# Seven products for the queries and keys of the second branch, and another placing of the weight sums

## The chip, the cores and the metric

The kernel runs on one core of one Trainium2 chip. The metric is the device time of one execution in microseconds (us), lower is better. One matmul step of the source (`nc.tensor.matmul` on fp32) stands in the trace as two MATMUL instructions.

## What is computed

Two layers of a transformer-like step on 640 tokens (512 latent, 128 context) of width 1024. Each layer forms modulation vectors, projects the modulated input h with one large matrix, runs three attention branches, gates and merges them, and ends with a mixture of experts. What this case touches:

```python
mod = jax.nn.silu(cvec) @ w_mod_l + b_mod_l            # 6 x 1024 values, twice (context, latent)
h = x * (1.0 + sc1) + sh1
qa, ka, va, qb, kb, vb, qc, kc, vc = split(h @ w_in_l)  # qb, kb: 512 columns each
ga, gb, gc = split(sigmoid(h @ w_gate_l + b_gate_l), 3)
y = (ga * (oa @ w_br_l[0]) + gb * (ob @ w_br_l[1]) + gc * (oc @ w_br_l[2])) @ w_o_l
```

## The kernel before

**Stages.** Per layer, for each branch `br` in 0, 1, 2: `project(br)` (chunks of `h @ w_in`, `CHUNKS`: 2, 0, 1, then 3, 4, 5, then 6, 7), `attend(br)` (18 slots of scores, softmax, transposes and value products) and `merge` (the branch's output product, gated into zT by VectorE at L2519). TensorE fills the gaps of the attention with the products of the gate `h @ w_gate`; `FILL` says how many steps stand in each slot.

**Seven products.** A gate pair has 2 blocks of 128 outputs, 1024 inputs and 640 tokens: halves in each direction, 2 x 2 x 2, so eight products of 4 steps in the plain way. `fill` makes it seven (LOW_LOW, CROSS, HIGH_LOW, DOWN, ACROSS, LATE, HIGH_HIGH, 4 steps of 320 columns each): GpSimd makes sums of token halves (`token_sum`, L1061), VectorE makes four sums of weight quarters per pair (`first_sums`: L2320 to L2322, `last_sum`: L2328) and adds the products from PSUM (`add_products`, L2350 to L2359, one 128x320 instruction or two each). The weights of LATE are made in place in `cross_sum`, once CROSS has read it; the first sums of the next pair wait for LATE.

**Chunks 3 and 4** (queries and keys of branch 1) are computed turned, features on the partitions: `units(c)` is 8, each unit is 8 steps of 320 columns (64 steps a chunk), and ScalarE copies each unit to `QT` or `KT`. Chunk 5 (values) is five units of 8 steps of 512 columns.

**Modulation.** Two groups of 8 pieces of `w_mod` (1 MB each) are summed per layer by VectorE while chunks 3 to 5 run: `modulation_partials`, two passes of 128x2048 a piece (L2368 for the first piece of a group, L2370 for others), 32 in all. After 16 passes TensorE sums the partials over partitions (`sum_partials`, L1246), once after unit (4, 1) and once after (5, 3).

**Order around the change.** SyncE loads 1 MB pieces in program order (L984) into a ring of six slots, each as soon as the piece that held the slot is used; `PROJECT_SLOTS` and `MOD_ORDER` place those of branch 1, and the modulation pieces have two slots. Every engine's own order is written out by hand; an engine waits in order, so what stands behind a waiting instruction waits too. In a slot s of `attend`, VectorE does maxima(s), gate work, the branch's output copy, and the softmax end of s; scores(s + 1) wait for ScalarE's exponentials of s, and the value product of item 1, 5, 9 and 13 waits for the output copy (v_oev) of the unit before.

Of the kernel before, what the change touches and what calls it, by code (L numbers as in the profile page):

```python
# [24 lines left out]
CTX = LAT  # L25
# [30 lines left out]
SIGMOIDS = 3  # L56
PIECE = 2048
# [262 lines left out]
def turned(c):  # L320

    return c in (3, 4)


def units(c):

    return 8 if turned(c) else NT
# [19 lines left out]
def build_kernel(nc, A, OUT):  # L347
# [14 lines left out]
    with ctx:  # L362
# [72 lines left out]
        part_sum = area(26624, 512).rearrange("p (k n) -> p k n", k=4)  # L435
        cross_sum = sb("cross_sum", [128, 4, 128])
        cexp = area(18176, KB * 32).rearrange("p (k n) -> p k n", k=KB)
# [158 lines left out]
        v_sum, g_gated = sem("outputs_summed"), sem("outputs_gated")  # L596
# [29 lines left out]
        class SumsDone:  # L626


            def __init__(self, first, last):
                self.first, self.last, self.done = first, last, [[0, 0] for _ in range(3)]  # L630

            def upto(self, br, n):
                done = self.done[br]
                while True:
                    a, b = done
                    if a > b:
                        if SEVEN * b + CROSS + 1 > n:
                            return
                        self.last(br, b)
                        done[1] += 1  # L640
                    else:
                        if a == PAIRS or (a and SEVEN * (a - 1) + LATE + 1 > n):
                            return
                        self.first(br, a)
                        done[0] += 1
# [315 lines left out]
        for layer in range(DEPTH):  # L961
# [3 lines left out]
            with nc.Block(no_gpsimd_drain=True) as block:  # L965
# [60 lines left out]
                def _(pool):  # L1026
# [35 lines left out]

                    for br in range(3):
# [11 lines left out]
                        if br == 1:  # L1075
# [6 lines left out]
                            if layer == 0:  # L1082
                                zero_row = y_all[0:1, :].rearrange("r (p n) -> (r p) n", p=8)
                                pool.dma_start(zero_row, MB[0:8, 0, MB_ZERO[0]:MB_ZERO[0] + 128]).then_inc(zero_out, 16)
                            for g in range(LAT):
                                masked_bias(0, g)
                            load_bias(1)
                        if br == 2:
                            token_sum(2, 3)
                        for c in CHUNKS[br]:  # L1090
# [11 lines left out]
                            i = PU.index((br, c, CTX))  # L1102
                            typ = CHUNK_TYPE[c]
                            if typ == "k" and turned(c):

                                pool.wait_ge(a_copy, AU.index(PU.index((br, c, units(c) - 1))) + 1)
# [91 lines left out]
                def _(pe):  # L1198
# [40 lines left out]
                    def sum_partials(g):  # L1239
# [4 lines left out]
                        for v in range(2):  # L1244
                            for j in range(STRIPS):
                                last = nc.tensor.matmul(ps[32 * j:32 * j + 32, 6, :], unit_col[:, v, :], mod_acc[:, v, 512 * j:512 * j + 512],  # L1246
# [76 lines left out]

                    def project(br):
                        for n, c in enumerate(CHUNKS[br]):
# [4 lines left out]
                            if layer and br == 0 and n == 0:  # L1330
                                own_outputs(pe, layer - 1)
                                transpose_x(0, 4)
                            for t in range(units(c)):
                                i = PU.index((br, c, t))
                                if br and (n, t) == (0, 2):

                                    pe.wait_ge(v_z, KB * br)
                                if i >= 4:
# [6 lines left out]
                                for k in range(KB):  # L1345
# [10 lines left out]
                                    if turned(c):  # L1356
                                        b, part = divmod(t, 2)
                                        last = mm(ps[:, bank_of(i), 0:320], wk[:, 128 * b:128 * b + 128], hT[:, k, 320 * part:320 * part + 320],
                                                  k == 0, k == KB - 1, frees=k < KB - 1)
                                        continue  # L1360
# [6 lines left out]
                                if (c, t) in MOD_SUMS:  # L1367
                                    sum_partials(1 + MOD_SUMS.index((c, t)) + (layer == 0))
# [1853 lines left out]
```

## Time and profile before

| | us |
|---|---|
| median of 3 runs | 2136.37 (2136.27 to 2140.67) |
| the profiled execution's own time | 2136.38 |
| its span in the trace | 2134.3 |
| TensorE busy (matmul) | 2007.2, 94% |
| VectorE busy | 1292.1, 61% |
| ScalarE busy | 513.9, 24% |
| GpSimd busy | 238.2, 11% |

TensorE is near saturated over the whole span. The mean granted clock of TensorE is 0.984 of full speed. The trace gives each engine's instructions with their start, their length and, in brackets, how long the engine had been idle before and what ended that.

### The profile page before, as it was taken

The numbers are of one execution on the slowest core, as the hardware profiler recorded it, in microseconds if no ns is written. First come the engines' busy times: TensorE is split into PE (matmuls) and PEld (weight loads), VectorE is DVE, ScalarE is ACT, GpSimd is POOL, SyncE is SP. The second block draws the span as 40 slices with busy tenths as digits, with TensorE's granted clock in tenths as the row PEclk, the third lists the DMA queues.
The fourth block names the chain that finished last, engine by engine and source line by source line (L and its number), as shares of the span: only waits on it lengthen the run. The fifth ranks groups of instructions, "written<-read, shape, count | busy, mean of one in ns | idle before, by whom it ended". The sixth has DMA issues, their size and how long they took to land. (4 is left out here: it accounts for less than half of the span.)

```text
span 2134.3 us, 25339 instructions
## 1 busy us (share of the span) xinstructions
PE 2007.2 (94%) x9546; PEld 1173.9 (55%) x9546; DVE 1292.1 (61%) x2031; ACT 513.9 (24%) x1007; POOL 238.2 (11%) x250
## 2 busy tenths in 40 slices
PE   7999999999999999699899999999999999979995
PEld 3457766566467754344244676656755676434432
DVE  2747747675456665756444574776744665866664
ACT  2114401143124400122130342003402342002221
POOL 1000020421110000100120002031101000010003
PEclk9999999999999999899999999999999999989998
DMA  7631046411120061689781111552111105238996
GB/s 284 243 118 40 21 143 222 138 55 44 40 82 21 33 279 79 247 341 362 257 278 48 64 41 64 195 185 87 48 57 46 43 21 221 105 133 322 385 350 199
DMA packets 62682, 317.00 MB, mean 149 GB/s; under 512 B 14824, under 2 KB 15280, under 8 KB 34272
## 3 DMA queue, kind: packets, MB, share of 16 engines
q1 hardware_dynamic: 32688, 232.41, 28.9%
q0 software_dynamic: 13136, 53.64, 7.7%
q10 hardware_dynamic: 16736, 29.32, 3.8%
q8 instruction: 77, 1.26, 0.2%
q14 instruction: 45, 0.37, 0.0%
HBM read 286.70 MB, written 27.07 MB: 147 GB/s over the span
## 5 line engine op out<-in xcount | busy, mean ns | idle before, releaser
L1217 PE MATMUL ps<-ring,hT 128*128 128x512 f32 (+1 forms) x960 | 388.4, 560 | 4.0 <-DVE hT L2190 2.0
L1217 PE MATMUL ps<-ring,zT 128*128 128x512 f32 (+2 forms) x992 | 317.5, 600 | 2.0 <-ACT zT L2093 2.0
L1217 PE MATMUL ps<-R,ring 128*128 128x512 f32 (+2 forms) x1024 | 292.3, 437 | 6.3 <-DVE zT L2522 3.5
L1217 PEld LDWEIGHTS ps<-ring,hT 128*128 128x128 f32 x960 | 179.4, 191 | 187.4 <-issue 176.7
L1217 PE MATMUL ps<-hT,ring 128*128 128x320 f32 x896 | 260.5, 436 | 0.0
L1217 PEld LDWEIGHTS ps<-R,ring 128*128 128x128 f32 x1024 | 161.9, 191 | 118.0 <-issue 92.8
L1217 PEld LDWEIGHTS ps<-ring,zT 128*128 128x128 f32 (+2 forms) x992 | 121.5, 156 | 149.0 <-issue 146.4
L1217 PEld LDWEIGHTS ps<-hT,ring 128*128 128x128 f32 x896 | 164.8, 190 | 65.2 <-issue 2.6
L2370 DVE SCALAR_TENSOR_TENSOR R<-ring,cs,R 128x2048 f32<-128x2048 f32 x70 | 173.3, 2476 | 8.3 <-DMA ring<-in_wall 5.5
L2025 ACT COPY R<-ps 128x512 f32<-128x512 f32 (+2 forms) x170 | 96.1, 565 | 271.3 <-PE ps L1506 253.8
L1445 PE MATMUL ps<-R 64*128 64x128 f32 (+2 forms) x992 | 123.2, 374 | 5.7 <-ACT R L1896 2.5
L1445 PEld LDWEIGHTS ps<-R 64*128 64x128 f32 x992 | 92.1, 186 | 38.5 <-ACT R L2011 12.0
L1217 PE MATMUL ps<-ring,R 128*128 128x320 f32 (+3 forms) x304 | 106.6, 530 | 2.5 <-issue 1.5
L2011 ACT ACTIVATE R<-ps,nmax 128x640 f32<-128x640 f32 x128 | 100.4, 789 | 6.2 <-DVE nmax L2410 4.4
L2410 DVE TENSOR_REDUCE nmax<-ps 128x2 f32<-128x1280 f32 x64 | 95.5, 1491 | 9.0 <-PE ps L1445 6.2
L1506 PE MATMUL ps<-ident,R 128*128 128x128 f32 x648 | 87.7, 273 | 7.1 <-DVE R L2431 4.2
L1506 PEld LDWEIGHTS ps<-ident,R 128*128 128x128 f32 x648 | 76.7, 141 | 30.1 <-DVE R L2431 6.3
L2440 DVE RECIPROCAL rinv<-rsum 128x2 f32<-128x2 f32 x96 | 15.9, 166 | 113.4 <-ACT R L2011 112.8
L1039 POOL TENSOR_TENSOR small<-small,half 128x4 f32<-128x4 f32 (+2 forms) x30 | 33.6, 1118 | 404.8 <-DVE small L2240 237.6
L2521 DVE SCALAR_TENSOR_TENSOR R<-R,ps 128x640 f32<-128x640 f32 x32 | 26.3, 821 | 84.1 <-PE ps L1217 83.7
L1543 PE MATMUL ps<-R 128*64 128x128 f32 x1024 | 70.5, 279 | 4.0 <-DVE R L2458 2.0
L1543 PEld LDWEIGHTS ps<-R 128*64 128x64 f32 x1024 | 54.5, 136 | 31.8 <-ACT R L2025 16.9
(335 smaller groups left out, 2460.8 us busy)
## 6 DMA issues: line engine op xcount, KB each, us to landing
ring<-in_wall SPq DMA_DIRECT2D x188, 1024.0 KB, 6.0
hT<-in_wall SPq DMA_DIRECT2D x20, 1024.0 KB, 8.9
y_all<-R ACTq DMA_DIRECT2D x27, 512.0 KB, 6.9
R<-in_wall SPq DMA_DIRECT2D x10, 1024.0 KB, 9.0
R<-in_rows POOLq DMA_DIRECT2D x2, 4096.0 KB, 17.9
R<-mrows POOLq DMA_DIRECT2D x16, 512.0 KB, 21.5
R<-in_x ACTq DMA_DIRECT2D x10, 512.0 KB, 8.9
h_rows<-R ACTq DMA_DIRECT2D x10, 512.0 KB, 2.6
```

The source lines that it names most:

```text
L1039: ch.step(nc.gpsimd.tensor_tensor(dst, src, half[:, 0:dst.shape[1]], ALU.pow), g_sq)
L1217: ins = nc.tensor.matmul(out, w, m, start=start, stop=stop, **kw)
L1445: return nc.tensor.matmul(out, QT[lo:lo + 64, b, 128 * r:128 * r + 128], KT[lo:lo + 64, key_slot(br, b), k0:k0 + n], start=True, stop=True)
L1506: last = nc.tensor.transpose(ps[:, 3 + c + k // 4, 128 * (k % 4):128 * (k % 4) + 128], P[:, i % 2, c, 128 * k:128 * k + 128], ident[:])
L1543: last = nc.tensor.matmul(ps[64 * a:64 * a + 64, 5, 128 * r:128 * r + 128], values[:, 64 * vh:64 * vh + 64], PT[:, a, 128 * j:128 * j + 12 ...
L2011: ins = nc.scalar.activation(dst, src, ACT.Exp, bias=nmax[:, n + a:n + a + 1], accum_out=rsum[:, n + a:n + a + 1])
L2025: ch.step(nc.scalar.copy(dst, src), a_pt)
L2370: ins = V_.scalar_tensor_tensor(mod_acc[:, v], w, c, mod_acc[:, v], ALU.mult, ALU.add)
L2410: ch.step(V_.tensor_reduce(nmax[:, n:n + 2].unsqueeze(2), src, axis=AX.X, op=ALU.max, negate=True), v_max)
L2440: ch.step(V_.reciprocal(rinv[:, o:o + 2], rsum[:, n:n + 2]), v_rinv)
L2521: ch.step(V_.scalar_tensor_tensor(g, g, 1.0, src, ALU.add, ALU.mult), v_chain)
```

## The change

- Chunks 3 and 4 become four pairs of seven products (`turned_pair`): 112 steps of 320 columns instead of 128. The token sums are those that GpSimd made for branch 0's gate, still in place. The four weight sums of a pair go to **GpSimd** (`sum_turned`), VectorE adds the products (`add_turned`, 6 instructions of 128x320 a pair), and ScalarE copies only LOW_LOW and HIGH_LOW. Every product has its own bank, so it waits for the same product's add of the pair before.
- The modulation passes are dealt out: 7 behind the gating steps of branch 0, 19 behind product adds (`PASSES`), 6 after them. The first group's partials are kept in an area of their own (`first_acc`). Its sum on TensorE comes after pair 1 (`FIRST_SUMMED`). `MOD_ORDER` is (4, 4, 0): four modulation pieces are loaded between chunks 3 and 4.
- In the gates, the weights of LATE are written over the weight piece's first quarter, once LOW_LOW has read it; the next pair's first sums wait for ACROSS, not LATE; and VectorE does at most two sums in a slot (`MOST_SUMS`), one at a time.

```diff
-MOD_ORDER = ((2, 6, 0), (0, 0, 8))
-MOD_SUMS = ((4, 1), (5, 3))
+MOD_ORDER = ((4, 4, 0), (0, 0, 8))
+MOD_SUMS = ((3, 3), (5, 3))
+FIRST_SUMMED = 1
+PASSES = ((1, 1, 1, 1, 1), (1, 1, 1, 1, 0), (1, 1, 1, 1, 1), (1, 1, 1, 1, 1))
-PROJECT_SLOTS = (0, 1, 2, 3, 4, 5) + 3 * (2, 3) + (0, 1) + 4 * (2, 3)
+PROJECT_SLOTS = (0, 1, 2, 3, 2, 3, 4, 5, 2, 3, 2, 3, 0, 1) + 4 * (2, 3)
...
+            def upto(self, br, n, most):
+                while most and self.done[br] < SUMS * PAIRS:
+                    p, j = divmod(self.done[br], SUMS)
+                    if n < (SEVEN * p + LOW_LOW + 1 if j == SUMS - 1 else SEVEN * (p - 1) + ACROSS + 1 if p else 0):
+                        return
+                    self.one(br, p, j)
+                    self.done[br] += 1
+                    most -= 1
...
+                    def sum_turned(q):
+
+                        for i in turned_pieces(layer, q):
+                            pool.wait_ge(full[slot_of(layer, i)], 16 * loads_by(layer, i))
+                        if q >= 2:
+                            pool.wait_ge(pe_acc, turned_no(q - 2, HIGH_HIGH))
+                        (a11, a12), (a21, a22) = turned_weights(layer, q)
+                        both, cross, far = turned_sums[q % 2]
+                        ch.step(nc.gpsimd.tensor_tensor(both, a21, a22, ALU.add), g_turn)
+                        ch.step(nc.gpsimd.tensor_tensor(cross, both, a11, ALU.subtract), g_turn)
+                        ch.step(nc.gpsimd.tensor_tensor(a21, a11, a21, ALU.subtract), g_turn)
+                        ch.step(nc.gpsimd.tensor_tensor(far, a12, cross, ALU.subtract), g_turn)
...
+                            sum_turned(0)
+                            pool.wait_ge(pe_gate, gate_no(0, PAIRS - 1, LATE))
+                            pool.wait_ge(v_anorm, NT)
+                            sum_turned(1)
                             for g in range(LAT):
                                 masked_bias(0, g)
                             load_bias(1)
+                            for q in range(TILE_PAIRS, TURNED_PAIRS):
+                                sum_turned(q)
...
+                            if turned(c):
+                                for q in range(TILE_PAIRS * (c - 3), TILE_PAIRS * (c - 2)):
+                                    turned_pair(q)
+                                    if q == FIRST_SUMMED:
+                                        sum_partials(1 + (layer == 0), first_acc)
+                                used(2)
+                                continue
...
-                            modulation_partials()
+                            for q in range(TURNED_PAIRS):
+                                for o, n in zip((CROSS, DOWN, ACROSS, LATE, HIGH_HIGH), PASSES[q]):
+                                    add_turned(q, o)
+                                    partials(n)
+                            partials(4 * KB)
                             gate_sums(1, 0)
...
-                        dve.wait_ge(pe_gate, gate_no(br, p, CROSS))
-                        ch.step(V_.tensor_tensor(cross_sum[:], w[:, high, 0:128], cross_sum[:], ALU.subtract), g_sum)
+                            dve.wait_ge(pe_gate, gate_no(br, p, LOW_LOW))
+                            ch.step(V_.tensor_tensor(a11, a12, cross_sum[:], ALU.subtract), g_sum)
...
+                    def add_turned(q, o):
+
+                        dve.wait_ge(pe_acc, turned_no(q, o))
+                        if o == CROSS:
+                            dve.wait_ge(a_copy, AU.index(PU.index((1, 3, 0))) + 2 * q + 1)
+                        got = ps[:, TURNED_BANKS[o], 0:320]
+                        _, second, third_, fourth = turned_quarters(q)
+                        scale = HD ** -0.5 if q < TILE_PAIRS else 1.0
+                        for out, acc, sign in {CROSS: ((fourth, fourth, 1.0),), DOWN: ((third_, fourth, 1.0),),
+                                               ACROSS: ((second, fourth, 1.0), (fourth, third_, 1.0)), LATE: ((second, second, 1.0),),
+                                               HIGH_HIGH: ((third_, third_, -1.0),)}[o]:
+                            ch.step(V_.scalar_tensor_tensor(out, got, sign * scale, acc, ALU.mult, ALU.add), v_turn)
...
-                                    gate_sums(br, products_by(br, s - 1, 2))
+                                    gate_sums(br, products_by(br, s - 1, 2), MOST_SUMS)
...
                                 ch.step(V_.scalar_tensor_tensor(g, g, 1.0, src, ALU.add, ALU.mult), v_z)
+                                if m < KB - 1:
+                                    partials(1)
```

On VectorE, from the last gating step of branch 0 (128x640) to the first gate sums of branch 1, layer 0, before:

```order
L2519 SCALAR_TENSOR_TENSOR zT<-zT,ps 128x640 x8
L2368 TENSOR_SCALAR R<-ring,cs 128x2048 x2
L2370 SCALAR_TENSOR_TENSOR R<-ring,cs,R 128x2048 x14
L2368 TENSOR_SCALAR R<-ring,cs 128x2048 x2
L2370 SCALAR_TENSOR_TENSOR R<-ring,cs,R 128x2048 x14
L2320 TENSOR_TENSOR R<-ring 128x512
```

and now, the end of pair 1 and the start of pair 2 of the turned products:

```order
L2524 SCALAR_TENSOR_TENSOR R<-ps,R 128x320 x2
L2490 SCALAR_TENSOR_TENSOR R<-ring,cs,R 128x2048
L2524 SCALAR_TENSOR_TENSOR R<-ps,R 128x320
L2490 SCALAR_TENSOR_TENSOR R<-ring,cs,R 128x2048
L2524 SCALAR_TENSOR_TENSOR R<-ps,R 128x320 x2
L2488 TENSOR_SCALAR R<-ring,cs 128x2048
L2524 SCALAR_TENSOR_TENSOR R<-ps,R 128x320
L2488 TENSOR_SCALAR R<-ring,cs 128x2048
```

A block of 32 passes without a product has become passes with product adds (L2524) between them; the first group's last pass (the second L2490 here) stands behind pair 1's LATE, and the second group's first pass (L2488) behind pair 2's CROSS.

On GpSimd, between branch 0's attention and the token sums (L1061 before, L1097 now) of branch 1, before:

```order
L1056 TENSOR_TENSOR R<-R,mask 128x256 x8
L1043 DMA R<-in_bias 128x2x384
L1107 DMA out_bk<-R 512x1x128
L1061 TENSOR_TENSOR ring<-hT 128x1280
```

and now, the part behind the second pair's sums:

```order
L1092 TENSOR_TENSOR R<-R,mask 128x256 x8
L1079 DMA R<-in_bias 128x2x384
L1107 TENSOR_TENSOR R<-ring 128x512
L1108 TENSOR_TENSOR R<-R,ring 128x512
L1109 TENSOR_TENSOR ring<-ring 128x4x128
L1110 TENSOR_TENSOR R<-ring,R 128x512
L1107 TENSOR_TENSOR cross_sum<-ring 128x512
```

Sixteen sums of 128x512 are new, eight of them ahead of the bias sums and eight (the last four are not shown) behind, between the projection's products.

On VectorE in slot 2 of branch 0's attention, layer 0, before (L2410 maxima, L2466 to L2240 the output unit's copy and squares, L2440 to L2445 the end of the softmax):

```order
L2410 TENSOR_REDUCE nmax<-ps 128x2
L2466 TENSOR_TENSOR R<-ps,cinv 128x512
L2238 TENSOR_TENSOR R<-R 128x512
L2239 TENSOR_REDUCE small<-R 128x4
L2240 TENSOR_SCALAR small<-small 128x4
```

and now:

```order
L2553 TENSOR_REDUCE nmax<-ps 128x2
L2441 TENSOR_TENSOR R<-ring 128x512
L2443 TENSOR_TENSOR cross_sum<-R,ring 128x512
L2609 TENSOR_TENSOR R<-ps,cinv 128x512
L2350 TENSOR_TENSOR R<-R 128x512
L2351 TENSOR_REDUCE small<-R 128x4
```

The first two sums of gate pair 1 (L2441, L2443) stand in slot 2, ahead of the output copy; they stood in slot 3.

## Rows read from the trace of the kernel before

**Rows 1.** Page, busy us (share), instructions of an engine:

```profile
PE 2007.2 (94%) x9546; PEld 1173.9 (55%) x9546; DVE 1292.1 (61%) x2031; ACT 513.9 (24%) x1007; POOL 238.2 (11%) x250
```

**Rows 2.** Timeline of TensorE, branch 1's projection, layer 0; start, length, instructions merged:

```profile
301.29 43.23 PE L1217 MATMUL ps<-hT,ring 128*128 128x320 f32 x160
344.45 1.92 PE L1246 MATMUL ps<-R 128*32 128x512 f32 x16
...
399.81 1.92 PE L1246 MATMUL ps<-R 128*32 128x512 f32 x16
```

**Rows 3.** Timeline of VectorE, the same stretch; idle before and releaser in brackets:

```profile
302.44 2.61 DVE L2368 TENSOR_SCALAR R<-ring,cs 128x2048 f32<-128x2048 f32 x2
...
309.99 9.51 DVE L2370 SCALAR_TENSOR_TENSOR R<-ring,cs,R 128x2048 f32<-128x2048 f32 x4 [0.17 <-DMA ring<-in_wall]
...
366.48 25.34 DVE L2370 SCALAR_TENSOR_TENSOR R<-ring,cs,R 128x2048 f32<-128x2048 f32 x8 [2.69 <-DMA ring<-in_wall]
404.69 0.69 DVE L2320 TENSOR_TENSOR R<-ring 128x512 f32<-128x512 f32 x1 [12.88 <-DMA mrows<-R]
```

**Rows 4.** Timeline, GpSimd's token sums, and one VectorE pass beside them:

```profile
376.80 4.43 POOL L1061 TENSOR_TENSOR ring<-hT 128x1280 f32<-128x1280 f32 x1 [2.83 <-DMA out_bk<-R]
381.31 4.81 POOL L1061 TENSOR_TENSOR ring<-hT,ring 128x1280 f32<-128x1280 f32 x1
...
383.41 4.86 DVE L2370 SCALAR_TENSOR_TENSOR R<-ring,cs,R 128x2048 f32<-128x2048 f32 x1
...
386.20 7.01 POOL L1061 TENSOR_TENSOR ring<-hT 128x640 f32<-128x640 f32 x2
```

**Rows 5.** Timeline of GpSimd, token sums of layer 1:

```profile
1421.43 4.61 POOL L1061 TENSOR_TENSOR ring<-hT 128x1280 f32<-128x1280 f32 x1 [5.38 <-DMA out_bk<-R]
...
1431.01 3.14 POOL L1061 TENSOR_TENSOR ring<-hT 128x640 f32<-128x640 f32 x2
```

**Rows 6.** Timeline, VectorE reading PSUM beside GpSimd:

```profile
275.18 6.33 POOL L1056 TENSOR_TENSOR R<-R,mask 128x256 f32<-128x256 f32 x8 [2.45 <-DMA R<-in_bias]
...
279.95 0.82 DVE L2519 SCALAR_TENSOR_TENSOR zT<-zT,ps 128x640 f32<-128x640 f32 x1 [3.71 <-PE ps L1217]
...
432.93 0.49 DVE L2357 TENSOR_TENSOR R<-R,ps 128x320 f32<-128x320 f32 x1
```

**Rows 7.** SyncE's loads; stretch: its us, engines busy, clock, DMA share, GB/s:

```profile
305.08 0.33 SPq L984 DMA_DIRECT2D ring<-in_wall  x1
...
336.47 0.33 SPq L984 DMA_DIRECT2D ring<-in_wall  x1
...
348.00:350.00 2.00, 2.00 (x9) 1.42 (x8) 1.96 (x2) 0.00 (x0) 0.00 (x0) 1.00 0.05 16
```

**Rows 8.** Timeline of TensorE, branch 1's attention: starts of slots, one wait:

```profile
434.79 0.92 PE L1445 MATMUL ps<-R 64*128 64x256 f32 x8
...
440.28 1.32 PE L1217 MATMUL ps<-ring,cross_sum 128*128 128x320 f32 x4 [1.56 <-issue]
...
442.33 0.92 PE L1445 MATMUL ps<-R 64*128 64x256 f32 x8
...
448.08 0.92 PE L1445 MATMUL ps<-R 64*128 64x256 f32 x8
```

**Rows 9.** Timeline of TensorE, waits in slots of branches 0 and 2:

```profile
206.01 1.31 PE L1217 MATMUL ps<-R,cross_sum 128*128 128x320 f32 x4 [0.83 <-DVE cross_sum L2321]
...
671.85 0.44 PE L1543 MATMUL ps<-R 128*64 128x128 f32 x4 [1.01 <-DVE R L2458]
```

**Rows 10.** Timeline, branch 0's slot 3: exponentials on ScalarE, next scores on TensorE:

```profile
172.90 0.80 ACT L2011 ACTIVATE R<-ps,nmax 128x640 f32<-128x640 f32 x1 [0.54 <-DVE nmax L2410]
...
174.69 0.70 PE L1445 MATMUL ps<-R 64*128 64x128 f32 x3
```

**Rows 11.** TensorE after a gap, and a stretch with its clock (third from last):

```profile
26.15 5.40 PE L1217 MATMUL ps<-ring,hT 128*128 128x512 f32 x8 [2.03 <-DVE hT L2190]
...
27.00:28.00 1.00, 1.00 (x2) 0.33 (x1) 0.81 (x2) 0.65 (x2) 0.00 (x0) 0.50 0.96 401
```

More of the change, by code:

```diff
@@ L56 @@
 SIGMOIDS = 3
+MOST_SUMS = 2
 PIECE = 2048
@@ L322, in turned @@
     return c in (3, 4)
+TILE_PAIRS = 2
+TURNED_PAIRS = 4
+TURNED_BANKS = (2, 3, 2, 4, 5, 0, 1)
 def units(c):
-    return 8 if turned(c) else NT
+    return 2 * TILE_PAIRS if turned(c) else NT
 def lat(i):
@@ L626, in build_kernel, with __init__, turned_pieces, pieces_index @@
         class SumsDone:
[L629 to L645, printed above, removed]
+            def __init__(self, one):
+                self.one, self.done = one, [0] * 3
+            def upto(self, br, n, most):
[6 more added lines that the diff above has]
+                    most -= 1
+        def turned_pieces(layer, q):
+            return [pieces_index(layer, ("in", 3 + q // TILE_PAIRS, h)) for h in range(2)]
+        def pieces_index(layer, what):
+            return STREAM[layer].index((layer, what))
+        def turned_weights(layer, q):
+            b = 2 * (q % TILE_PAIRS)
+            tiles = [slot_at(slot_of(layer, i)).rearrange("p (k n) -> p k n", k=4) for i in turned_pieces(layer, q)]
+            return [[w[:, :, 128 * m:128 * m + 128] for w in tiles] for m in (b, b + 1)]
+        def turned_quarters(q):
+            b, both = 2 * (q % TILE_PAIRS), (QT, KT)[q // TILE_PAIRS]
+            return (both[:, b, early], both[:, b, late], both[:, b + 1, early], both[:, b + 1, late])
+        def turned_no(q, o):
+            return PU.index((1, 3, 0)) + SEVEN * q + o + 1
+        def turned_adds(q, o):
+            return ADDS * q + (0, 1, 1, 2, 4, 5, 6)[o]
+        def acc_no(i):
+            return i + 1 + (SEVEN * TURNED_PAIRS - 2 * units(3) if PU[i][1] >= 5 and PU[i][0] else 0)
         class Chain:
@@ L1322, in first_units, with turned_pair @@
                         used(1 if h else 1 + KB // 2)
+                    def turned_pair(q):
+                        for h in range(2):
+                            take("in", h)
+                        (a11, a12), (a21, a22) = turned_weights(layer, q)
+                        both, cross, far = turned_sums[q % 2]
+                        copied = AU.index(PU.index((1, 3, 0))) + 2 * q
+                        for o in range(SEVEN):
+                            if o == LOW_LOW:
+                                if q:
+                                    pe.wait_ge(a_copy, copied)
+                                weights, tokens = a11, lambda k: hT[:, k, early]
+                            elif o == CROSS:
+                                if q:
+                                    pe.wait_ge(v_turn, turned_adds(q - 1, CROSS))
+                                pe.wait_ge(g_turn, SUMS * q + 2)
+                                weights, tokens = cross, lambda k: token_row(layer, 0, 1, k)
+                            elif o == HIGH_LOW:
+                                pe.wait_ge(a_copy, copied + 1)
+                                weights, tokens = a12, lambda k: hT[:, 4 + k, early]
+                            elif o == DOWN:
+                                if q:
+                                    pe.wait_ge(v_turn, turned_adds(q - 1, DOWN))
+                                pe.wait_ge(g_turn, SUMS * q + 3)
+                                weights, tokens = a21, lambda k: token_row(layer, 0, 2, k)
+                            elif o == ACROSS:
+                                if q:
+                                    pe.wait_ge(v_turn, turned_adds(q - 1, ACROSS))
+                                weights, tokens = both, lambda k: token_row(layer, 0, 0, k)
+                            elif o == LATE:
+                                if q:
+                                    pe.wait_ge(v_turn, turned_adds(q - 1, LATE))
+                                else:
+                                    pe.wait_ge(v_z, KB)
+                                pe.wait_ge(g_turn, SUMS * q + 4)
+                                weights, tokens = far, lambda k: hT[:, 4 + k, late]
+                            else:
+                                if q:
+                                    pe.wait_ge(v_turn, turned_adds(q - 1, HIGH_HIGH))
+                                weights, tokens = a22, lambda k: token_row(layer, 0, 3, k)
+                            for k in range(STEPS):
+                                last = mm(ps[:, TURNED_BANKS[o], 0:320], weights[:, k, :], tokens(k), k == 0 and o != HIGH_LOW, k == STEPS - 1,
+                                          frees=k < STEPS - 1, skip_group_check=o in (LOW_LOW, HIGH_LOW))
+                            last.then_inc(pe_acc, 1)
@@ L2290, in project @@
                             for t in range(NT):
+                                if turned(c):
+                                    continue
                                 i = PU.index((br, c, t))
@@ new lines, in _, with partials @@
+                    passes = modulation_passes()
+                    def partials(n):
+                        for _ in range(n):
+                            next(passes, None)
+                    def add_turned(q, o):
[9 more added lines that the diff above has]
+                            ch.step(V_.scalar_tensor_tensor(out, got, sign * scale, acc, ALU.mult, ALU.add), v_turn)
```

97 lines of the change are left out of this document (56 added, 41 removed).

## The prediction

> **What bounds the kernel now.** I read the page first, then the timeline of each engine for the stages that the change touches, then the waits that end last there. The page: TensorE is busy for 94% of the span, VectorE for 61% [rows 1]. So a removed TensorE instruction is worth its whole length, unless another engine becomes late. In branch 1's projection TensorE runs without a break: 43.2 us for 160 instructions, 0.27 us each, then the first sum of the partials, and so on to the second sum at 399.8 [rows 2]. VectorE is the engine nearest to it there: 32 passes, done at 391.8 (366.48 + 25.34), 8 us before TensorE asks for them [rows 3, 2]. It has 8 us of cover over a stage of 98.5 us, and the change wants to take 8.6 us off TensorE and put work on VectorE. In the attention TensorE works too, but some slots are longer than their neighbours: one of branch 1 takes 7.54 us (434.79 to 442.33), the next 5.75, and in the first stands a wait of 1.56 us ahead of CROSS, whose weights VectorE's sums had not yet made [rows 8].
>
> **TensorE's saving.** A step of 320 columns is two instructions, 0.54 us. Four pairs save 4 steps each: 16 x 0.54 = **8.6 us per layer**, 17.2 in all, if nothing else is late. I call T the start of the stage (301.3). A product takes 2.16 us, a pair 15.1, so pair 1 ends at T+30.3, and without any wait the second sum would start at T + 60.5 + 1.9 + 27.5 = T+89.9 (27.5 us for four units of chunk 5, the 399.8 of [rows 2] less the end of the turned units), against T+98.5 before.
>
> **VectorE up to the first sum.** A pass costs 2.38 us (9.51 / 4), the four single-input ones of the two groups 1.31 (2.61 / 2) [rows 3]; a product add is not in the trace in this form, but 128x320 with one PSUM operand takes 0.49, and the same form at 640 columns 0.82 [rows 6], so 0.52 with its gap. The seven passes behind the gating steps are free: such a step stands behind 3.71 us of idle time [rows 6], and the eight of a layer are alike. From DOWN of pair 0 on (T+8.6) VectorE has, up to the 16th pass, 10 adds (5.2) and 8 passes (19.1): T+33.1, 2.8 after TensorE. GpSimd comes on top. Its sums and the passes exclude each other: the token sum issued at 381.31 ends at 386.12, the pass issued at 383.41 ends at 388.27, that is 2.15 after it, and the next token sums get in only behind it [rows 4]. So each waits for the other's whole instruction, one after the other. An instruction with a PSUM operand is not held: 0.82 beside GpSimd's eight sums and 0.82 where it is alone [rows 6], so a product add can run under a weight sum. A 128x512 sum on GpSimd I take at 1.27 us (0.8 of the 1.57 of 640 columns [rows 5]). GpSimd starts pair 2's sums at T+15.1, and four or five of them fall between these passes, 1.15 each less the 0.52 to 1.04 of adds under them: +2.0. The 16th pass ends at T+35.1, and TensorE **waits 4.8 to 5 us**. Bounds: 2.8 (the sums cost nothing) and 7.2 (one more sum gets in ahead of the last two passes).
>
> The Trainium skill (GPSIMD Engine Reference, section Engine selection) speaks against putting these sums on GpSimd: two-input work is about 2x slower there than on VectorE. The trace agrees (1.27 by scaling against 0.69). By the skill's factor a sum would be an estimated 1.38 us, and the first wait would come out some 0.5 us longer; the sum below goes by the scaled rows.
>
> **VectorE from there to the second sum.** The first sum takes 1.9, so pair 2 starts at T+37.1. Its first passes need the first piece of the second group, and this load now stands in SyncE's queue behind the two loads of chunk 5, which need chunk 3's slots, freed by pair 2's first steps. Before, the burst of four such loads began at 336.47, 0.7 us into the unit after chunk 3 (16 x 0.27 x 8 = 34.5 us behind 301.29), and was over at 348 [rows 7, 2]: 12.2 us into that unit, so three of the four take until about 9.7 (a quarter of the 10 us of transfer less). A load alone takes 4.9 (305.08 to 309.99) [rows 7, 3]. So pass 17 starts 9.7 us into pair 2, not 4.8. A gap of TensorE also has a price: after 2.03 us of idle time the granted clock was 0.50, the level of 1.2 GHz, and 8 instructions took 5.4 us, 2.0 more than at 0.43 each [rows 11]. Behind the wait of 5 us pair 2 runs slow at first; the loads go out some 1.3 us later. Pass 17 at T+48.1. Then 2 passes at 1.31, 14 at 2.38, 11 adds at 0.52: 41.8; and GpSimd's token sums, which start when pair 3 is added up and the new keys are out (3.9 us after the last copy in layer 0), now meet the last five passes instead of the last three: 2.74 + 2.74 + 1.42 + 1.42 + 2.07 less 0.2 for each pass that follows at once = 9.4 [rows 4]. The 32nd pass ends at **T+99.3**. TensorE alone would be there at T+96.9. So layer 0's second sum is 0.8 us later than before. In layer 1 the wait for the keys' store is 5.4 where it was 2.8 [rows 5, 4], so 1.8 us less of the token sums meet the passes: T+97.5, **1.0 us earlier**. Whether the 2.4 us gap in layer 0 halves the clock again (0 to 2.0) I can't say; I take 1.0. Projection, both layers: 0.8 - 1.0 + 1.0 = **+0.8 us**. The saving of 17.2 is eaten by VectorE.
>
> Free, with their cover: ScalarE's copies (8 instead of 16 per layer), the earlier bias load, the four modulation pieces ahead of chunk 4 (chunk 4's own loads go out 35 us before their use), the first eight weight sums (under the output product).
>
> **The weight sums in the attention.** I went through the slots whose length is above their branch's. Branch 1, layer 0: the CROSS of pair 1 finds its weights made one slot earlier, the slot falls from 7.54 to 5.75: -1.8, and about -0.1 elsewhere [rows 8]. Branch 2: the wait of 1.01 for the third chunk's copy, behind three sums and an output copy, goes, the slot is 1.1 shorter; nothing else [rows 9]. Branch 0: the wait of 0.83 goes, -1.07 with what hangs on it [rows 9]. But pair 1's first two sums now stand in slot 2, ahead of the output copy and the chain of the norm: 2 x 0.72 = 1.45 us [rows 3], and slot 3 has none to spare, since ScalarE waits for the maxima there (0.54), begins the exponentials at 172.90, and the next scores follow them at once, at 174.69 [rows 10]: **+1.45**. The last pair's late weights join an output in slot 14: +0.4. Branch 0 is +0.8, the layer 0.8 - 1.9 - 1.15 = -2.25, both layers **-4.5 us**. The change of the place of LATE's weights costs nothing by itself: the instruction is the same, one operand lies in the ring.
>
> **Sum.** 2136.38 (the profiled execution, 0.01 from the median) - 4.5 + 0.8 = 2132.7; I write **2132.5**, rounding to the side of the bounds below, of which more lie under it. That is 0.18% faster, near the edge of what a measurement here tells from no change (0.2%, 4.3 us).
>
> **Rivals.**
> (a) VectorE's stage is shorter than I walked it: GpSimd's sums slip in where it idles, or the load lands early. With only the 2.8 us wait and nothing at the second sum, it starts at T+92.7, 5.8 earlier per layer: 2136.4 - 4.5 - 11.6 = 2120.3; with half of it 2126. For it: VectorE has some 10 us of idle time around pair 2's start. Against: what follows is a chain without a gap. 0.28.
> (b) VectorE's stage is longer, the slower side. Place: pass 17 and what it waits for. If the piece lands at 12 us instead of 9.7 (one load of this stretch made VectorE wait 2.69 [rows 3]) and each gap halves the clock (2.0), both layers lose 0.8 + 2.3 + 2.0 = 5.1 or near it: 2136.4 - 4.5 + 10.2 = 2142.1. It decides from the point where the 32nd pass ends later than T+103. 0.11.
> (c) The attention gives nothing: each sum that is moved finds another wait, as in branch 0's slot 2. Then 2136.4 + 0.8 = 2137. 0.12.
> (d) The forecast, 2129 to 2136: 0.49.
>
> **How the numbers follow.** Faster by over 0.2% (below 2132.1): 0.21 of (d), 0.27 of (a): 0.48. Within 0.2%: 0.28 of (d), 0.11 of (c), 0.02 of (b), 0.01 of (a): 0.42. Slower (above 2140.6): 0.09 of (b), 0.01 of (c): 0.10. The range reaches half into (a) and up to where (b) begins: 2123 to 2140. The forecast's own range is 2129 to 2136.
>
> **What would show it.** The trace after: 224 turned instructions per layer, pairs of 15.1 us; TensorE idle ahead of the first sum of partials by 3 to 7 us, released by VectorE's pass; the granted clock at 0.50 behind it; VectorE idle for about 10 us ahead of the second group's first pass, released by a load; the second sum 97 to 100 us after T; passes of up to 4.8 us beside GpSimd; the 7.54 us slot at 5.75 and branch 0's slot 3 longer by 1.4. If the first wait is under 2 us or the second sum comes before T+94, (a) holds and my view of the exclusion is wrong.

## The result and the profile after

| | us |
|---|---|
| kernel before, median of 20 runs | 2135.95 |
| changed kernel, median of 20 runs | 2139.22 |
| ratio, 95% interval | 1.0017 (1.0010 to 1.0024) |
| changed kernel's profiled execution, its span | 2135.48, 2133.7 |

The changed kernel is 3.3 us slower by the medians and 3.6 by the ratio, where I had forecast 3.9 us faster. The time lies in my range, the direction was wrong. Its profiled execution is the shortest of its 20, 3.7 us under their median, and one reading has to be made ahead of all others. The first eight matmuls behind the first gap, in the changed kernel's profiled execution and, in the second fence, in another execution of the same kernel (start, length, [idle before]):

```profile
26.48 3.70 PE L1272 MATMUL ps<-ring,hT 128*128 128x512 f32 x8 [2.16 <-DVE hT L2302]
```

```profile
25.84 5.40 PE L1272 MATMUL ps<-ring,hT 128*128 128x512 f32 x8 [1.59 <-DVE hT L2302]
```

The same work took 3.70 us behind the longer gap and 5.40 behind the shorter one, as before [rows 11]. So this execution was spared a stretch at half clock that others pay. Its span must not be compared with that of before; its stages can be.

Page of the changed kernel, beside [rows 1]:

```profile
PE 1994.6 (93%) x9482; PEld 1162.3 (54%) x9482; DVE 1335.7 (63%) x2079; ACT 507.6 (24%) x991; POOL 330.1 (15%) x282
```

TensorE has 64 instructions less. GpSimd has 92 us more of busy time for 32 more instructions; at 1.27 us each, what one takes alone, they would be 41 us, and much of the rest is waiting, as will be seen. TensorE in branch 1's projection, layer 0, where T = 300.58, to be read against [rows 2]:

```profile
300.58 2.32 PE L1272 MATMUL ps<-hT,ring 128*128 128x320 f32 x8
...
336.02 3.55 PE L1301 MATMUL ps<-R 128*32 128x512 f32 x16 [5.12 <-DVE R L2490]
339.49 2.42 PE L1272 MATMUL ps<-hT,ring 128*128 128x320 f32 x8
...
401.56 3.21 PE L1301 MATMUL ps<-R 128*32 128x512 f32 x16 [4.18 <-DVE R L2490]
404.69 7.13 PE L1272 MATMUL ps<-ring,hT 128*128 128x512 f32 x16
```

TensorE waits 5.12 us ahead of the first sum and 4.18 ahead of the second. Both sums, 1.92 us before, take 3.55 and 3.21: the stretches 336:339 and 402:404 have a granted clock of 0.50, the level of 1.2 GHz. The second sum starts at T+101.0; before it was T+98.5. In layer 1 (T = 1342.48):

```profile
1377.92 3.64 PE L1301 MATMUL ps<-R 128*32 128x512 f32 x16 [5.12 <-DVE R L2490]
1381.49 3.56 PE L1272 MATMUL ps<-hT,ring 128*128 128x320 f32 x8
...
1444.64 3.09 PE L1301 MATMUL ps<-R 128*32 128x512 f32 x16 [4.14 <-DVE R L2490]
1447.66 7.62 PE L1272 MATMUL ps<-ring,hT 128*128 128x512 f32 x16
```

Here the half clock behind the first wait reaches into pair 2's first product (3.56 for 2.42 in layer 0). The second sum starts at T+102.2, and its half clock reaches into the next unit (7.62 for 7.13). VectorE in layer 0, with the second group's first pass and the last four:

```profile
344.16 0.49 DVE L2524 SCALAR_TENSOR_TENSOR R<-ps,R 128x320 f32<-128x320 f32 x1 [7.67 <-PE ps L1272]
350.54 1.29 DVE L2488 TENSOR_SCALAR R<-ring,cs 128x2048 f32<-128x2048 f32 x1 [5.88 <-DMA ring<-in_wall]
...
385.34 16.16 DVE L2490 SCALAR_TENSOR_TENSOR R<-ring,cs,R 128x2048 f32<-128x2048 f32 x4
```

VectorE idles 13.6 us in two waits, first for TensorE's next product, then for the load of pass 17, 11.05 us into pair 2. What follows is a chain without a gap to 401.50.

Counted from slot to slot over both layers, before and after: the three attention stages gained 4.5 us, the projection with what its clock does lost 9.0 (3.7 in layer 0, 5.3 in layer 1). That is +4.5, where the 20 runs have +3.3 by the medians (2.1 to 5.1 by the interval of the ratio).

### The profile page after: what moved, and what is told of

Same layout as the page of the kernel before. It is cut to its first block and busy times, and to the rows that moved or that the text cites. A ratio compares the mean times of both kernels' runs of the same rounds, so it can differ in the third digit from the quotient of the medians.

```text
span 2133.7 us, 25334 instructions
## 1 busy us (share of the span) xinstructions
PE 1994.6 (93%) x9482; PEld 1162.3 (54%) x9482; DVE 1335.7 (63%) x2079; ACT 507.6 (24%) x991; POOL 330.1 (15%) x282
## 5 line engine op out<-in xcount | busy, mean ns | idle before, releaser
L1272 PE MATMUL ps<-R,ring 128*128 128x512 f32 (+2 forms) x1152 | 329.4, 437 | 6.0 <-DVE zT L2667 3.2
L1272 PEld LDWEIGHTS ps<-R,ring 128*128 128x128 f32 x1152 | 186.2, 190 | 127.8 <-issue 92.8
L1272 PE MATMUL ps<-hT,ring 128*128 128x320 f32 x704 | 221.7, 441 | 0.2
L2490 DVE SCALAR_TENSOR_TENSOR R<-ring,cs,R 128x2048 f32<-128x2048 f32 x70 | 191.1, 2729 | 2.6
L1272 PEld LDWEIGHTS ps<-hT,ring 128*128 128x128 f32 x704 | 125.8, 191 | 48.5 <-issue 6.6
L1552 PEld LDWEIGHTS ps<-R 64*128 64x128 f32 x992 | 92.1, 186 | 40.8 <-ACT R L2123 13.6
L1272 PE MATMUL ps<-R 128*128 128x320 f32 (+3 forms) x224 | 77.2, 482 | 0.0
L1092 POOL TENSOR_TENSOR R<-R,mask 128x256 f32<-128x256 f32 x64 | 58.7, 917 | 111.3 <-DVE R L2552 70.7
```

What stands on the lines that cost most here:

```text
L1092: ch.step(nc.gpsimd.tensor_tensor(o, w, m, ALU.add), g_mb)
L1272: ins = nc.tensor.matmul(out, w, m, start=start, stop=stop, **kw)
L1552: return nc.tensor.matmul(out, QT[lo:lo + 64, b, 128 * r:128 * r + 128], KT[lo:lo + 64, key_slot(br, b), k0:k0 + n], start=True, stop=True)
L2490: ins = V_.scalar_tensor_tensor(acc[v], w, c, acc[v], ALU.mult, ALU.add)
```

## The experiments

Every kernel ran beside the kernel before (medians 2134.8 to 2136.0). The ratio is to that kernel. The last column is read from the traces: the time from the last scores of branch 0 to the first of branch 1, which holds branch 1's projection, for both layers together. It was 315.2 us in the kernel before and 324.2 in the changed kernel's first trace. The changed kernel's two traces differ by 0.2 us in this sum (by up to 0.9 in a single layer), where its whole executions scatter by 9 us, so the column shows small effects more surely than the medians do.

| kernel | median us | ratio, 95% interval | projection stage, us |
|---|---|---|---|
| changed, again | 2138.99 | 1.0016 (1.0007 to 1.0025) | 324.0 |
| projection alone | 2143.18 | 1.0039 (1.0024 to 1.0053) | 324.2 |
| attention alone | 2132.59 | 0.9983 (0.9971 to 0.9995) | 315.2 |
| TensorE kept busy | 2136.60 | 1.0005 (0.9997 to 1.0014) | 317.8 |
| kept busy in the waits only | 2133.50 | 0.9990 (0.9979 to 1.0000) | 317.5 |
| load order | 2130.91 | 0.9983 (0.9972 to 0.9994) | 316.0 |
| sum after pair 2 | 2134.91 | 0.9997 (0.9984 to 1.0009) | 320.2 |
| short GpSimd sums | 2130.81 | 0.9981 (0.9969 to 0.9993) | 316.2 |
| areas apart | 2118.05 | 0.9908 (0.9887 to 0.9930) | 301.8 |
| areas apart, slot 2 free | 2112.89 | 0.9894 (0.9875 to 0.9913) | 301.8 |
| the same, a pass earlier | 2111.59 | 0.9886 (0.9871 to 0.9901) | 297.9 |

**The two halves of the change.** First the changed kernel with the old `first_sums` and `last_sum`:

> The changed projection with the weight sums of the gates as they were before. Theory 1 (the attention gives its 4.5 us, and the projection loses what the two profiles show, 3.7 us in layer 0 and 5.3 in layer 1, since the second group's first pass starts 11 us into pair 2 and each wait of TensorE is followed by a stretch at half clock): about 2144, 7.5 to 9 us above the kernel before. Rival (the projection costs the 0.8 us that I forecast and the attention loses 2.5): 2137.

Then the kernel before with the new ones:

> The kernel before with the changed weight sums of the gates alone (LATE's weights in the piece's first quarter, at most two sums in a slot). Theory 1: slot 2 of branch 0 longer by 1.25, slot 8 shorter by 1.06, slot 4 of branch 1 shorter by 1.79, slot 6 of branch 2 shorter by 1.11, in both layers, so 4.5 us below the kernel before, 2131.5. Rival (the attention gives nothing or loses): 2136 to 2138.5.

By the ratios the projection alone costs 8.3 us (5.1 to 11.3), as theory 1 has it, and excludes the rival. The attention alone gains 3.6 (1.1 to 6.2). Its trace has each slot where I had put it: branch 0's slot 2 7.61 us for 6.38, slot 8 6.38 for 7.44, branch 1's slot 4 5.75 for 7.54, branch 2's slot 6 6.63 for 7.74. In the changed kernel the scores of branch 1's slots 4 and 5 start 5.75 us apart, against the 7.54 of [rows 8]:

```profile
437.82 0.92 PE L1552 MATMUL ps<-R 64*128 64x256 f32 x8
443.57 0.92 PE L1552 MATMUL ps<-R 64*128 64x256 f32 x8
```

and this is the new wait in branch 0's slot 2 (L2609 is the output copy):

```profile
166.54 1.35 PE L1647 MATMUL ps<-R 128*128 128x128 f32 x10 [1.01 <-DVE R L2609]
```

**The half clock.** TensorE is given work in its waits, overwritten by the sum:

```diff
-                        pe.wait_ge(v_freed, KB * g)
                         if n_mod[0]:
                             pe.wait_ge(a_mod, n_mod[0])
+                        for _ in range(8 if acc is first_acc else 6 if acc_after else 0):
+                            nc.tensor.matmul(ps[:, 6, 0:320], ident[:], hT[:, 0, 0:320], start=True, stop=True)
+                        pe.wait_ge(v_freed, KB * g)
```

> The changed kernel with TensorE at work in most of its two waits: 8 products of 320 columns into the bank of the sum ahead of the wait for the first group's last pass (4.3 us of the 5.1), 6 ahead of the second group's (3.2 of the 4.1). The first of the sum's matmuls overwrites them. Theory A (the half clock behind the waits is part of the loss, and what comes behind moves with it): the first sum takes 1.9 us and not 3.5, pair 2 and the load for pass 17 come 1.6 us earlier in layer 0 and up to 3 in layer 1, the second sum takes 1.9 and not 3.1: 6 to 7 us below the changed kernel, 2132 to 2133. Rival B (VectorE's chain and the load set the second sum's time whatever TensorE's clock): only the second wait's 1.3 to 1.8 us a layer, 2136.

Its median, 2136.60, is the rival's number. But that kernel also had six products ahead of a third sum, in branch 0's projection, where there is no wait to fill: 3.3 us of pure addition, which neither theory had counted. Its projection stage of branch 1 is 6.3 us shorter than the changed kernel's. Without the six:

> As the first kernel with TensorE kept busy, without the 6 products that this one also had ahead of a sum in branch 0's projection of layer 0, where there is no wait (3.3 us there). Theory A (clock): 2132.6 to 2133.5, 6 to 7 us below the changed kernel; the second sum at T+99.3 in layer 0 (it was T+101.0) and T+100.3 in layer 1 (T+102.2). Rival B (the first one gained by something else and loses it here): 2136.

Its TensorE in layer 0 (T = 301.51) and layer 1 (T = 1343.25):

```profile
336.95 1.92 PE L1303 MATMUL ps<-R 128*32 128x512 f32 x16 [0.82 <-DVE R L2492]
...
400.69 1.92 PE L1303 MATMUL ps<-R 128*32 128x512 f32 x16 [0.78 <-DVE R L2492]
...
1443.44 1.92 PE L1303 MATMUL ps<-R 128*32 128x512 f32 x16 [1.77 <-DVE R L2492]
```

VectorE is no earlier for the first sum, yet the sums take 1.92 us, the second starts at T+99.2 and T+100.2, and the kernel is 5.5 us faster than the changed one (2133.50 to 2138.99 on one chip; some 3 to 8 by the intervals). The stage is 6.6 us shorter. So of the projection's loss of 9.0 us, 60 to 75% was TensorE's clock behind waits that it had not had before, and what came later for it.

**The load.** Two pieces of the second group go ahead of chunk 5's:

```diff
-MOD_ORDER = ((4, 4, 0), (0, 0, 8))
+MOD_ORDER = ((4, 4, 0), (0, 2, 6))
-PROJECT_SLOTS = (0, 1, 2, 3, 2, 3, 4, 5, 2, 3, 2, 3, 0, 1) + 4 * (2, 3)
+PROJECT_SLOTS = (0, 1, 2, 3, 2, 3, 4, 5, 2, 3, 2, 3, 2, 3, 0, 1) + 3 * (2, 3)
```

> The changed kernel with two pieces of the second modulation group loaded ahead of chunk 5's two. Theory A (pass 17 was late because its load stands behind chunk 5's in SyncE's queue): pass 17 starts right behind the first sum, at T+39.5 and not T+50.0, the 32nd pass ends near T+91, the second sum starts at T+97 without a wait and at full clock: 4 to 5 us a layer for the start and 1.3 to 1.8 for the clock, in all 11 to 13 us below the changed kernel, 2126 to 2128; the wait of 5.1 us ahead of the first sum stays. Rival B (passes held up by GpSimd are the cause and the load only fills idle time): 32nd pass moves by less than 3 us, 2134 or above.

8.1 us below the changed kernel by the medians (some 4 to 10 by the intervals), and 8.1 in the stage: less than theory A said, more than B. Its VectorE shows the rest (T = 301.24):

```profile
344.76 0.49 DVE L2524 SCALAR_TENSOR_TENSOR R<-ps,R 128x320 f32<-128x320 f32 x1 [7.60 <-PE ps L1272]
345.29 1.29 DVE L2488 TENSOR_SCALAR R<-ring,cs 128x2048 f32<-128x2048 f32 x1
349.08 0.49 DVE L2524 SCALAR_TENSOR_TENSOR R<-ps,R 128x320 f32<-128x320 f32 x1 [2.51 <-PE ps L1272]
```

Pass 17 waits no longer for its load, but it stands behind the add of pair 2's CROSS, and this product is done 4.6 us after the first sum. It started at T+44.1, not at T+39.5, and each product ahead of a pass held VectorE again. The second sum came at T+98.6 and T+99.3 behind a wait of 1.86 us, at full clock.

**GpSimd.** Its sums of pairs 2 and 3 are made on 4 of 512 columns (half the queries' and keys' heads are then another function):

```diff
-                        ch.step(nc.gpsimd.tensor_tensor(both, a21, a22, ALU.add), g_turn)
+                        some = slice(0, 1 if q >= TILE_PAIRS else 128)
+                        def part(a):
+                            return a[:, :, some]
+                        ch.step(nc.gpsimd.tensor_tensor(part(both), part(a21), part(a22), ALU.add), g_turn)
...
```

> The changed kernel in which GpSimd makes the weight sums of pairs 2 and 3 on 4 columns only instead of 512 (the rest of these weights is left as it was, so queries and keys of half the heads are another function of h). Theory A (each pass and each of these sums wait for each other's whole length, as the prediction took them, +2.0 us on the first wait): the wait ahead of the first sum falls from 5.1 to 3.1, with all behind it 2 us earlier, 4 us in all, 2135. Rival B (GpSimd's sums cost VectorE nothing, the product adds lie under them): the wait stays at 4.6 to 5.1, 2138 to 2139.

GpSimd's sums of pair 2 in the changed kernel, where one alone takes 1.27:

```profile
316.01 1.26 POOL L1107 TENSOR_TENSOR R<-ring 128x512 f32<-128x512 f32 x1 [14.32 <-PE ps L1272]
317.35 3.20 POOL L1108 TENSOR_TENSOR R<-R,ring 128x512 f32<-128x512 f32 x1
320.63 3.20 POOL L1109 TENSOR_TENSOR ring<-ring 128x512 f32<-128x512 f32 x1
323.91 3.20 POOL L1110 TENSOR_TENSOR R<-ring,R 128x512 f32<-128x512 f32 x1
```

and TensorE's first wait with the short sums, layers 0 and 1:

```profile
335.04 1.92 PE L1304 MATMUL ps<-R 128*32 128x512 f32 x16 [2.95 <-DVE R L2493]
...
1374.74 3.36 PE L1304 MATMUL ps<-R 128*32 128x512 f32 x16 [2.95 <-DVE R L2493]
```

The wait fell by 2.17 us to 2.95: theory A's term (3.1 expected). Each sum of 1.27 had waited out a VectorE pass, and held up the next one, which took 2.7 us for 2.35. The Trainium skill (SBUF — State Buffer, section SBUF: two separate sides) calls the pair of ports that the two engines share an exclusive lock for a whole instruction; the rows agree. The kernel gained 8.2 us by the medians (some 5 to 11 by the intervals) and 8.0 in the stage, twice what A said, since the clock came on top: in layer 0 the sum ran at full clock (1.92 us), and in layer 1 pair 2's first product did (2.42, where it had been 3.56).

**The first sum one pair later,** and nothing else:

```diff
-MOD_SUMS = ((3, 3), (5, 3))
-FIRST_SUMMED = 1
+MOD_SUMS = ((4, 1), (5, 3))
+FIRST_SUMMED = 2
```

> The changed kernel with the first sum of partials behind pair 2 instead of pair 1, nothing else. The second group's passes write where the first group's partials lie, so pass 17 waits for this sum. Theory A: no wait and no half clock ahead of the first sum (T+45.4), pass 17 at T+47.3, then a chain without a gap of 50.5 us: second sum at T+98 with a wait of about 8 us and half clock behind it. 3 to 4 us a layer earlier than in the changed kernel and one stretch at half clock less: 2131 (2129 to 2133). Rival B (the wait only moves from the first sum to the second): second sum still at T+101 to 102, 2139.

TensorE's second sum in both layers (T = 301.69 and 1343.80):

```profile
400.08 3.64 PE L1301 MATMUL ps<-R 128*32 128x512 f32 x16 [8.41 <-DVE R L2490]
...
1442.20 3.64 PE L1301 MATMUL ps<-R 128*32 128x512 f32 x16 [8.42 <-DVE R L2490]
```

T+98.4 in both, as A has it, but 4.1 us below the changed kernel (some 1 to 7 by the intervals; 4.0 in the stage) and not 8, outside the 2129 to 2133 that A gave: the one wait of 8.4 us is followed by more time at half clock (the next unit takes 8.32 and 7.80 for 7.13) than I had given it.

**All three taken away.** To the new load order come the first sum after pair 2 and areas of their own for the two groups:

```diff
-FIRST_SUMMED = 1
+FIRST_SUMMED = 2
-        first_acc = [area(5632, 2048), area(8704, 2048)]
+        first_acc = [area(5632, 2048), area(7680, 2048)]
+        second_acc = [area(9728, 2048), area(11776, 2048)]
-                            if n == KB:
-                                dve.wait_ge(pe_mod, 4 if layer == 0 else 1)
-                            acc = first_acc if n < KB else [mod_acc[:, v] for v in range(2)]
+                            acc = first_acc if n < KB else second_acc
```

(The load of the cached values of branch 1, whose place `first_acc` takes, waits for the first sum.)

> The changed kernel with the two pieces of the second modulation group loaded ahead of chunk 5's, the two groups' partials in areas of their own (so the second group's first pass waits for no sum; the cached values of the branch are loaded behind the first sum instead of ahead of it), and the first sum behind pair 2 instead of pair 1. Theory A (the loss was three waits in a row: TensorE for pass 16, pass 17 for the sum, for its load and for pair 2's products; passes and sums themselves fit): VectorE ends pass 32 at T+86 to T+90 without a gap of over 2 us, TensorE waits for neither sum and starts the second at T+90 to T+91, no half clock there: 11 us a layer below the changed kernel, 8 below the one before, with the attention's 4.5: 2114 to 2118. Rival B (VectorE's work with GpSimd's exclusion is itself too long for the stage): second sum at T+96 or later, 2126 or above.

16.7 us below the kernel before by the medians, 19.6 by the ratio (15 to 24), and theory A, though not to the end: the first sum has no wait, but the second starts at T+91.8 behind 1.86 us, where A had T+90 to T+91 and no wait (T = 303.79 in layer 0):

```profile
349.10 1.92 PE L1305 MATMUL ps<-R 128*32 128x512 f32 x16
...
395.63 1.92 PE L1305 MATMUL ps<-R 128*32 128x512 f32 x16 [1.86 <-DVE R L2494]
```

**Slot 2 of branch 0** keeps its output copy free:

```diff
-                                    gate_sums(br, products_by(br, s - 1, 2), MOST_SUMS)
+                                    gate_sums(br, products_by(br, s - 1, 2), 0 if (br, s) == (0, 2) else MOST_SUMS)
```

> As the kernel with the areas apart, and in slot 2 of branch 0's attention no weight sum, so that none stands ahead of that slot's output copy: pair 1's first two sums go to slot 3, the last two to slot 4. Theory A: slot 2 falls from 7.62 to 6.38 us and slot 8 stays at 6.38, so 2.5 us below the kernel with the areas apart. Rival B (the four sums now press slots 3 and 4): as much is lost there, no difference.

Scores of slots 2 and 3, 6.37 us apart; in the changed kernel they start at 160.21 and 167.83, 7.62 apart:

```profile
158.47 1.35 PE L1556 MATMUL ps<-R 64*128 64x128 f32 x10
164.84 1.35 PE L1556 MATMUL ps<-R 64*128 64x128 f32 x10
```

Slot 8 stays at 6.38, and branch 0's attention is 1.4 us shorter per layer, 2.8 in all. The medians differ by 5.2 us and the ratios by 3.0 where 2.5 were expected, on intervals of 4 us to either side: the slots show the size, the medians alone would not tell it from nothing.

**One pass moved ahead** of pair 3's products:

```diff
-PASSES = ((1, 1, 1, 1, 1), (1, 1, 1, 1, 0), (1, 1, 1, 1, 1), (1, 1, 1, 1, 1))
+PASSES = ((1, 1, 1, 1, 1), (1, 1, 1, 1, 0), (1, 1, 1, 1, 2), (1, 1, 1, 1, 1))
```

> As the kernel with both (areas apart, no sum in slot 2), with one more of VectorE's passes behind the last product add of pair 2, and so one less behind the last product of pair 3. Theory A (VectorE idles 0.9 and 1.4 us for pair 3's first products, and the passes left behind the last one set the second sum): the last wait of 1.86 us in both layers is under 0.5, 3 to 3.7 us below that kernel, about 2109.5. Rival B (the load of that pass is not there, or GpSimd's token sums set the end, T+91.8 stays): no difference, 2112 to 2113.

T = 300.13 and 1332.58:

```profile
390.04 1.92 PE L1305 MATMUL ps<-R 128*32 128x512 f32 x16
...
1422.48 1.92 PE L1305 MATMUL ps<-R 128*32 128x512 f32 x16
```

No wait in brackets: T+89.9 in both layers, TensorE's own time. The traces have the second sum 1.9 us earlier per layer and the stage 3.9 us shorter. The ratios of this kernel and the last (0.9886 and 0.9894) don't differ beyond their intervals, so the gain shows in the stage alone, not in the whole time. The stage is now 17.2 us shorter than in the kernel before, the whole of TensorE's saving. The changed kernel again, for its figure on the same chip as this kernel and the one kept busy in the waits only:

> The changed kernel once more, on the chip of these runs, to have its own figure beside them: 3.3 us above the kernel before, 2138 to 2139, and a granted clock of 0.978 to 0.980 where its profiled execution had 0.982.

It had 2138.99 and a clock of 0.979.

## Why the prediction was wrong

**Right.** TensorE's own time (T+89.9, seen once all waits were gone). The first wait of 4.8 to 5 us (5.12) and its parts: adds, passes, the exclusion by GpSimd (2.0 us forecast, 2.17 measured). (Its terms 8.6, 5.2 and 19.1 add up to T+32.9, where I wrote T+33.1; the trace has the first of these adds at T+8.9.) VectorE's chain from pass 17 to the 32nd pass in layer 0 (51.2 forecast, 51.0 measured). The attention, slot by slot: -4.5 forecast, -4.5 in the traces, with the loss in branch 0, though it falls in slot 2 itself, where a value product waits 1.01 us for the output copy, and not in slot 3.

**Wrong: the projection's +0.8 us, which was +9.0.** Four terms of it:
- *The load of pass 17, 9.7 us into pair 2.* Pass 17 started 11.05 us (layer 0) and 12.1 us (layer 1) into pair 2, and 10.8 and 11.9 us into it in the kernel kept busy in the waits, where pair 2 ran at full clock. That the third of four loads lands 2.5 us ahead of the last was right, but I had put the end of the burst at 348. In the trace before, the four loads landed 4.9, 6.8, 8.9 and 9.8 us after they were issued, that is at 341.3, 343.8, 346.3 and 348.8, so the third was there 10.5 us into the unit and not 9.7. In layer 1 of the kernel kept busy it landed 10.0 us after its issue, for 9.0 in layer 0; no run shows why.
- *The clock behind the first wait, 1.3 us.* The sum alone lost 1.6, and in layer 1 the first products of pair 2 as well. With the load it put pass 17 at T+50.0 and T+51.1, for a forecast of T+48.1: 1.9 and 3.0 us.
- *The clock behind the second wait,* which I left open in layer 0 (1.0 of 0 to 2.0) and did not count in layer 1, where I expected a wait of 0.6 us (T+97.5 against T+96.9). It cost 1.3 and 1.7: 0.3 and 1.7 more.
- *Layer 1's 1.8 us less of token sums,* from a wait of 5.38 us for the keys' store [rows 5]. I took it for a property of the layer and carried it over to another order of loads. With the new order it was 2.04 or 2.05 in both layers of the changed kernel and of six others. It goes with the loads beside the store. In layer 1 of the kernel before, the store was issued at 1415.3 and a load at 1415.5; the load landed at 1420.9 and the store at 1421.4. In the changed kernel the next load went out 1.8 us behind the store. One pass moved ahead, and with it the loads, took the wait from 2.25 to 4.13 (layer 0) and 3.98 (layer 1). That the store lands behind a load that is under way fits all these rows, but no run takes the load away. VectorE's chain in layer 1 took 51.0 us, as in layer 0, and not 49.4: 1.6 more.

Less 0.2 for the chain of layer 0, these terms add up to 8.3 us, for a miss of 8.2. By layers: 3.7 for a forecast of 1.8, and 5.3 for -1.0. What came was nearest to rival (b), the stage that is longer, to which I gave 0.11: its mechanism (the load lands at 12, each wait halves the clock) is the one that was there, with 9.0 us for the 10.2 I had worked out. Its sign, the 32nd pass behind T+103, did not come: the pass ended at T+100.9 and T+102.1. I had all its terms in rows and priced each at its middle in the forecast, though they are not independent. A later load makes a longer second wait, and behind each wait of 3.9 us or more the clock was halved here. Rival (a), with 0.28, rested on VectorE's idle time about pair 2; that idle time lay ahead of pass 17 and could not be used by anything, since the engine's order holds no other work there. Rival (c) fell: the attention gave what it should.

**What the change lacked.** Its saving of 17.2 us is real, and it comes out whole (T+89.9) once VectorE's passes of the second group wait neither for the first sum, nor for a load queued behind chunk 5's, nor for products that the first sum had held up. This version, 2111.59 us, beats the kernel before by 1.1%. I had listed the pass's load, but not that group 2's passes write over what the first sum reads: the area of `first_acc` is its own only in its first half; the second half begins at 8704, where the second group's `mod_acc` begins too, and a wait in the code holds pass 17 until the first sum is done. The experiments with the load alone and the sum alone (8.1 and 4.1 us of the 21 to the areas apart) show that each leaves the next wait in its place. The areas apart alone were not run, so how the other 9 us divide is not shown.

## What to carry to other kernels

- On a saturated TensorE, a new wait can cost more than its length: here each of 3.9 us or more was followed by 1.3 to 3.0 us lost to the half clock, while six waits of 1.86 us were not. Follow both through all that starts later. Where the wait itself can't go, products that are overwritten can bring the clock's part back (5.5 to 6.6 of the 9 us here).
- The second engine had 8 us of cover, and the change took 8.6 us of it away and added 12 us of adds (24 of 0.52). That looked like too little and was enough, since seven passes had moved ahead into idle time: with the three waits gone and one more pass moved, TensorE waited for neither sum. So ask which of the second engine's waits (area, load, order) keeps it from working ahead, and remove them together: each alone only uncovers the next.
- Loads that go out in a burst land one behind another, here 1 MB each 2.5 us. Read when the one you need lands, and not when the burst seems over. And a wait for a DMA that differs between two layers with the same work may be set by the loads beside it: don't carry it over to another order of loads.

## What the runs showed of the hardware

I had not expected that the length of a gap does not by itself tell whether the clock falls. At an early gap of TensorE, in a place that is the same in all thirteen profiled executions, eleven had the half clock behind 1.59 to 2.49 us of idle time (eight matmuls took 5.27 to 6.58 us), and two kept the full clock (3.70 us) behind 2.16 and 1.79. Behind the six waits of 1.86 ahead of second sums it stayed. After 2.95 us the sum ran at full clock in layer 0 (1.92) and at half clock in layer 1 (3.36). Each wait of 3.9 us or more shown here was followed by half clock.

This is a part of what moves one kernel's time from one execution to the next, but not all. The changed kernel's two traces differ by 2.4 us in their span: 0.9 us had come together up to the first scores (147.79 against 148.68), with the clock behind the first gap, and 1.8 us came between the last scores of layer 0 and the first of layer 1 (456.65 against 458.41). That stretch took 455.8 to 460.9 us in the thirteen traces; no run here shows why.
